# DeltaNet's triangular inverse: two value heads in one product per level, and where the transposes are made

## The reference, cut to what matters

```python
decay = jnp.exp(jnp.where(incl, gc[..., :, None] - gc[..., None, :], -jnp.inf))
kk = jnp.einsum("bhncd,bhnjd->bhncj", k, k)
m = jnp.where(strict, beta[..., :, None] * kk * decay, 0.0) + jnp.eye(C)
rhs = jnp.concatenate([v * beta[..., None], k * (beta * jnp.exp(gc))[..., None]], axis=-1)
sol = lax.linalg.triangular_solve(m, rhs, left_side=True, lower=True, unit_diagonal=True)
```

## Time and profile before

| | |
|---|---|
| time, median of 3 runs | 3418.48 us (3417.89 to 3418.68) |
| profiled execution, first to last instruction | 3413.1 us |
| PE busy | 3254.4 us, 95% |
| VectorE busy | 1421.6 us, 42% |
| ScalarE busy | 910.3 us, 27% |
| GpSimd busy | 1704.4 us, 50% |
| mean granted TensorE clock | 0.989 |

### The profile page before, as it was taken

How to read it: one execution, slowest core, us unless ns; L and a number is a source line. 1 busy time by engine, 2 the same in 40 slices (tenths; PEclk the granted TensorE clock), 3 DMA queues, 4 the chain that set the end, 5 groups by cost and what they waited for, 6 DMA issues and landing times.

```text
span 3413.1 us, 46693 instructions
## 1 busy us (share of the span) xinstructions
PE 3254.4 (95%) x16752; PEld 2712.9 (79%) x16752; DVE 1421.6 (42%) x1929; ACT 910.3 (27%) x1411; POOL 1704.4 (50%) x1748
## 2 busy tenths in 40 slices
PE   8999989999999999999999999999998999999996
PEld 7877878888888888888788887787777878778685
DVE  6722234333433343334331314333356565631723
ACT  5411133333333333333320102111113333310411
POOL 0255634433443344334326777765664555556684
PEclk9999999999999999999999999999999999999998
DMA  6322212211221122112224223222223222223222
GB/s 238 124 85 94 82 55 74 74 55 55 74 74 55 55 74 74 55 55 86 98 69 172 99 91 143 99 92 86 95 97 120 68 88 69 94 91 122 77 96 86
DMA packets 53530, 306.52 MB, mean 90 GB/s; under 512 B 5044, under 2 KB 7220, under 8 KB 21716
## 3 DMA queue, kind: packets, MB, share of 16 engines
q1 hardware_dynamic: 34528, 248.53, 21.2%
q10 hardware_dynamic: 18932, 57.00, 4.5%
HBM read 284.74 MB, written 20.77 MB: 90 GB/s over the span
## 4 chain that ended last, share of the span: by engine, by line
PE 80%; DVE 12%; ACT 5%; issue 2%; DMA 1%; ACTq 0%; DVEq 0%; SPq 0%
PE gemm_ps L436 19%; PE gemm_ps L438 19%; PE gemm_ps L437 19%; DVE arena L878 9%; PE bankC L580 4%; PE bankA L571 3%; ACT arena L1579 2%; PE gemm_ps L795 2%; DVE a_lo L878 2%; PE gemm_ps L797 2%; PE gemm_ps L796 2%; PE bankA L751 2%; PE bankB L587 1%; ACT a_hi L1579 1%; PE bankA L593 1%
## 5 line engine op out<-in xcount | busy, mean ns | idle before, releaser
L436 PE MATMUL gemm_ps<-a_hi,w_hi 128*128 128x512 f32 (+1 forms) x3472 | 1390.8, 401 | 15.4 <-DVE a_lo L878 13.4
L412 POOL CAST w_hi<-w_raw 128x512 fp32r<-128x512 f32 x872 | 547.2, 670 | 1661.9 <-issue 1504.2
L438 PE MATMUL gemm_ps<-a_hi,w_lo 128*128 128x512 f32 (+1 forms) x3472 | 1331.9, 384 | 0.0
L437 PE MATMUL gemm_ps<-a_lo,w_hi 128*128 128x512 f32 (+1 forms) x3472 | 1329.9, 383 | 0.0
L404 POOL TENSOR_TENSOR w_lo<-w_raw,w_hi 128x512 fp32r<-128x512 f32 x872 | 1161.0, 1363 | 4.2
L436 PEld LDWEIGHTS gemm_ps<-a_hi,w_hi 128*128 128x128 f32 x3472 | 657.5, 189 | 145.9 <-DVE a_lo L878 16.3
L438 PEld LDWEIGHTS gemm_ps<-a_hi,w_lo 128*128 128x128 f32 x3472 | 655.4, 189 | 131.2
L437 PEld LDWEIGHTS gemm_ps<-a_lo,w_hi 128*128 128x128 f32 x3472 | 657.5, 189 | 119.2 <-issue 9.0
L878 DVE TENSOR_TENSOR arena<-gemm_ps,arena 128x512 f32<-128x512 f32 (+3 forms) x161 | 107.1, 665 | 615.5 <-PE gemm_ps L438 496.3
L1579 ACT ACTIVATE arena<-arena 128x512 f32<-128x512 f32 (+5 forms) x350 | 214.6, 613 | 397.9 <-DVE arena L878 383.0
L878 DVE RECIPROCAL arena<-arena 128x512 f32<-128x512 f32 (+2 forms) x70 | 172.8, 2468 | 321.7 <-ACT arena L1579 319.7
(11 more groups left out here) (161 smaller groups left out, 2516.6 us busy)
## 6 DMA issues: line engine op xcount, KB each, us to landing
w_raw<-w_stream SPq DMA_DIRECT2D x236, 1024.0 KB, 4.9
y_scratch<-arena ACTq DMA_DIRECT2D x20, 512.0 KB, 3.4
arena<-y_scratch ACTq DMA_DIRECT2D x13, 512.0 KB, 4.3
arena<-gc_scratch ACTq DMA_DIRECT2D x12, 512.0 KB, 3.6
arena<-x_t ACTq DMA_DIRECT2D x2, 2048.0 KB, 10.1
arena<-y_scratch ACTq DMA_DIRECT2D x1, 4096.0 KB, 24.1
x_scratch<-arena ACTq DMA_DIRECT2D x1, 4096.0 KB, 15.7
y_out<-arena ACTq DMA_DIRECT2D x4, 1024.0 KB, 3.9
```

Source lines behind the costliest of these rows:

```text
L412: pool.tensor_copy(part(w_hi, w, q), part(w_raw, w, q)).then_inc(pool_step, 1)
L436: pe.matmul(o, hi, a_hi[:, k, 0:width], start=(k == 0), stop=False)
L437: pe.matmul(o, hi, a_lo[:, k, 0:width], start=False, stop=False)
L438: last = pe.matmul(o, lo, a_hi[:, k, 0:width], start=False, stop=(k == KT - 1))
```

## The change

The two heads share each level's two products. One combined 128x128 matrix per chunk, `pair_n`, holds one head's factor in one triangle and the other head's, transposed, in the other; `inv_b` and `inv_a` hold the pair's inverses in two arrangements. A row operand is brought on by VectorE: a block transposition (`v.transpose`, 128x512), a predicated copy with a mask per partition (`level_rows`) and a copy of the inner columns (`next_level`). TensorE transposes four matrices at three places only: beside the last "whole", in "turn" after level 5, and in "flip" after level 6. The head's scales move: the second head's values are scaled by `v_scale` when they are copied, `kd` and `ke` are made after levels 3 and 4, `dT` after level 1, and `ke` is waited for in "solved". `qd` comes first in "natural". A second reciprocal of `kroot` is kept in PSUM.

```diff
-DN_STEPS = ([("natural", 10), ("values", 8), ("transposed", 6)]
-            + [(s, l, a, w) for l in range(1, LEVELS - 1)
-               for s, a, w in (("half", 0, 0), ("half", 1, 0), ("whole", 0, 0), ("whole", 1, 1), ("turn", 0, 1),
-                               ("turn", 1, 1))]
-            + [(s, LEVELS - 1, a, w) for s, a, w in (("half", 0, 2), ("half", 1, 0), ("whole", 0, 1), ("whole", 1, 0))]
-            + [("solved", 6)]
+DN_STEPS = ([("natural", 12), ("values", 12)]
+            + [(s, l, w) for l in range(1, LEVELS - 2) for s, w in (("half", 1), ("whole", 4))]
+            + [("half", LEVELS - 2, 1), ("whole", LEVELS - 2, 1), ("turn", 3)]
+            + [("half", LEVELS - 1, 1), ("whole", LEVELS - 1, 2), ("flip", 2), ("solved", 4)]
             + [(s, n, g) for n in range(NB) for s, g in (("rest", 2), ("output", 3))]
-            + [("head_out", 28)])
+            + [("head_out", 18)])
...
+        pair_n, turned0 = Nm[:, 0, :, :], Nm[:, 1, :, :]
+        inv_b, inv_a = XT[:, 0, :, :], XT[:, 1, :, :]
+        half_t = T1[:, 0, :, :]
...
+        kinv_ps, ke_ps = (bankB[:, 1, NB * k:NB * k + NB] for k in range(2))
...
+                    pe.wait_ge(s["inv_ready"], 2 * level_count(j, l) - 1)
                     for n in range(NB):
-                        last = pe.matmul(quad(bankA)[:, a, n, :], NmT[:, a, n, :], X[:, a, n, :],
+                        last = pe.matmul(quad(bankA)[:, 0, n, :], pair_n[:, n, :], inv_a[:, n, :],
                                          start=True, stop=True)
...
+                    pe.wait_ge(s["t1_sbuf"], level_count(j, l))
+                    pe.wait_ge(s["inv_ready"], 2 * level_count(j, l))
                     if l == 1:
-                        pe.wait_ge(s["kd_ready"], j + 1)
+                        pe.wait_ge(s["vn_sbuf"], j + 1)
                     for n in range(NB):
-                        last = pe.matmul(quad(bankC)[:, a, n, :], T1[:, a, n, :], XT[:, a, n, :],
+                        last = pe.matmul(quad(bankC)[:, 0, n, :], half_t[:, n, :], inv_b[:, n, :],
                                          start=True, stop=True)
                     last.then_inc(s["dd"], 1)
+                    if l == LEVELS - 1:
+                        for n in range(NB):
+                            pe.transpose(quad(bankB)[:, 1, n, :], inv_a[:, n, :], ident)
+                elif step[0] in ("turn", "flip"):
+                    pe.wait_ge(s["lvl"], 3 * j + (1 if step[0] == "turn" else 2))
                     for n in range(NB):
-                        last = pe.transpose(quad(bankB)[:, a, n, :], XT[:, a, n, :], ident)
+                        last = pe.transpose(quad(bankC)[:, 1, n, :], inv_b[:, n, :], ident)
...
+            def level_rows(l, turned, j):
+                copy_after(v.copy_predicated, chunks(XT, 1), rows[:, l:l + 1].bitcast(U32).to_broadcast([P, T]), turned,
+                           sem=s["inv_ready"], value=2 * level_count(j, l + 1) - 1)
+            def next_level(l, j):
+                level_rows(l, bankC[:, 1, :], j)
+                op(v.tensor_copy, inner(chunks(XT, 0), l), inner(bankB[:, 1, :], l),
+                   sem=s["inv_ready"], value=2 * level_count(j, l + 1))
...
+                    v.wait_ge(s["dd"], level_count(j, l))
+                    late = l >= LEVELS - 2
+                    copy_after(v.copy_predicated, inv_b, both_ways[:, l:l + 1, :].to_broadcast([P, NB, P]),
+                               quad(bankC)[:, 0, :, :], sem=s["lvl"] if late else None, value=3 * j + l - LEVELS + 3)
+                    if late:
+                        return
+                    op(v.transpose, bankC[:, 1, :], chunks(XT, 0))
+                    next_level(l, j)
+                    op(v.transpose, bankB[:, 1, :], chunks(XT, 1))
                     if l == 1:
+                        op(v.tensor_tensor, dT[:, :, :, :], E[:, :, :, :], both(dTm), ALU.mult)
+                    elif l == 2:
+                        op(v.tensor_copy, ke_scale[:, :, 0], cb[:, :, 3, 0])
+                        op(v.tensor_scalar, u_scale[:, :, 0], neg_br[:, :, 0], -1.0, None, ALU.mult)
+                        op(v.tensor_copy, u_scale[:, :, 1], kroot)
+                        op(v.tensor_scalar, neg_k, kroot, -1.0, None, ALU.mult)
+                    elif l == 3:
+                        op(v.tensor_tensor, kd[:, :, :, :], both(by_chunk(bankB[:, 0, :])), by_row(kd_scale), ALU.mult)
                     else:
+                        op(v.tensor_tensor, ke[:, :, :, :], both(by_chunk(bankB[:, 0, :])), by_row(ke_scale), ALU.mult,
+                           sem=s["kd_ready"], value=j + 1)
...
-                    op(t1, t1_ps, ACT.Copy, s["t1_sbuf"], product_count(j, l, a))
+                    op(chunks(T1, 0), bankA[:, 0, :], ACT.Copy, s["t1_sbuf"], level_count(j, step[1]))
+                elif step[0] == "flip":
+                    act.wait_ge(s["turned"], 2 * j + 2)
+                    op(chunks(XT, 1)[0:P // 2, :], bankC[0:P // 2, 1, :], ACT.Copy, s["xt1"], j + 1)
```

More of the change, by code:

```diff
@@ L182, in build @@
         con = sb("con", [P, 4 + 2 * LEVELS, P])
-        ones, ident, incl, reset = (con[:, n, :] for n in range(4))
-        low = con[:, 4:4 + LEVELS, :].bitcast(U32)
+        ones, ident, incl, rows = (con[:, n, :] for n in range(4))
+        both_ways = con[:, 4:4 + LEVELS, :].bitcast(U32)
         lowT = con[:, 4 + LEVELS:4 + 2 * LEVELS, :].bitcast(U32)
@@ L241, in build @@
         kss, kroot, kinv = (at(o_ + 48 + NB * k, NB) for k in range(3))
-        neg_br, pos_br, neg_c, kd_scale = (at(o_ + 60 + 2 * NB * k, 2 * NB).rearrange("p (b a) -> p b a", a=2)
-                                           for k in range(4))
+        neg_br, neg_c, kd_scale, ke_scale, u_scale = (
+            at(o_ + 60 + 2 * NB * k, 2 * NB).rearrange("p (b a) -> p b a", a=2) for k in range(5))
+        v_scale, neg_k = (at(o_ + 60 + 10 * NB + NB * k, NB) for k in range(2))
         q_sq = root
-        assert o_ + 92 <= 20992
+        assert o_ + 60 + 12 * NB <= 20992
         xt = at(BASE, 8192).rearrange("p (k t) -> p k t", k=KT)
@@ L555, in dn_mix @@
                     last.then_inc(s["nat_v"], 1)
[L556 to L562, removed]
-                elif step[0] == "half":
[L564 to L569, removed]
+                elif step[0] == "half":
+                    l = step[1]
+                    pe.wait_ge(s["inv_ready"], 2 * level_count(j, l) - 1)
                     for n in range(NB):
-                        last = pe.matmul(quad(bankA)[:, a, n, :], NmT[:, a, n, :], X[:, a, n, :],
+                        last = pe.matmul(quad(bankA)[:, 0, n, :], pair_n[:, n, :], inv_a[:, n, :],
                                          start=True, stop=True)
@@ L1070, in dn_mix @@
                     op(v.tensor_tensor, neg_br, cb[:, :, 1, :], kinv2, ALU.mult)
                     op(v.tensor_tensor, neg_c, neg_br, kinv2, ALU.mult)
+                    op(v.tensor_scalar, v_scale, neg_br[:, :, 1], -1.0, None, ALU.mult)
                     v.wait_ge(s["pair"], j + 1)
-                    v.wait_ge(s["expd"], 2 * j + 1)
-                    for a in range(2):
+                    for a, to in ((1, pair_n), (0, quad(bankA)[:, 0, :, :])):
                         for n in range(NB):
-                            op(v.scalar_tensor_tensor, NmT[:, a, n, :], bankA[:, 0, n * P:n * P + P],
+                            op(v.scalar_tensor_tensor, to[:, n, :], bankA[:, 0, n * P:n * P + P],
@@ new lines, in dn_mix @@
+                    copy_after(v.copy_predicated, inv_b, both_ways[:, 0:1, :].to_broadcast([P, NB, P]), pair_n)
+                    op(v.transpose, chunks(Nm, 1), chunks(XT, 0))
+                    level_rows(0, chunks(Nm, 1), j)
+                    op(v.tensor_copy, inner(chunks(XT, 0), 0).rearrange("p (n b) t -> p n b t", n=NB),
+                       inner(ident, 0)[:, None, :, :].to_broadcast([P, NB, P // 4, 2]),
+                       sem=s["inv_ready"], value=2 * level_count(j, 1))
+                    op(v.tensor_tensor, kd_scale, cb[:, :, 2, :], kinv2, ALU.mult)
@@ L1083, in dn_mix @@
                            incl, ALU.mult, ALU.mult)
[L1084 to L1093, removed]
-                elif step[0] == "whole":
-                    l, a = step[1:3]
-                    v.wait_ge(s["dd"], product_count(j, l, a))
-                    if l == 1:
-                        changed = (XT[:, a, :, :], lowT[:, l:l + 1, :].to_broadcast([P, NB, P]), quad(bankC)[:, a, :, :])
-                    else:
-                        changed = (level_blocks(chunks(XT, a), l, 1), level_mask(lowT, l, 1),
-                                   level_blocks(bankC[:, a, :], l, 1))
-                    copy_after(v.copy_predicated, *changed, sem=s["lvl"], value=level_count(j, l, a))
@@ new lines, in dn_mix @@
+                elif step[0] == "whole":
+                    l = step[1]
+                    v.wait_ge(s["dd"], level_count(j, l))
[6 more added lines that the diff above has]
```

(23 more changed lines are left out.)

79 lines of the change are left out of this document (32 added, 47 removed).

## The result

The changed kernel takes 3314.69 us (median of 4 runs, 3310.75 to 3320.26) against 3418.18 before; ratio 0.9703, 95% interval 0.9689 to 0.9716. It is faster by 3.0%, and 69 us slower than the 3246 foreseen, outside the range. The profiled execution's span is 3311.8 us.

The account below looks back on a forecast made before the run. PE was taken as the bound, busy 95% of the span. Less PE work (176 us) and removed waits (51), minus new stalls (53) and a later last-trip start (2), gave 172 us off: 3246 us, range 3205 to 3295.

Parts of the forecast that it names:

- VectorE's own load: VectorE's operations summed per level: 5.4 us in level 1, 5.0 in levels 3 and 4, just under the chain's 5.5.
- four small ones together 0.8: Filler among VectorE's operations of a level: four small operations were priced at 0.8 us in all.
- the prediction's own 6.7 for level 2: VectorE from level 2's first copy_predicated through the second tile's convolution: 6.7 us, next result after 5.5, so 1.2 late.
- The trip of 98.5: One trip of the DeltaNet loop was to take 98.5 us after the change, against 113.3 before.
- The stalls: PE's new stalls, 4.4 us a trip, among them 0.5 at the turn, 0.7 for the last tile's convolution, 0.3 for `dT`.
- Fewer products: PE in each trip: 96 product instructions and 36 transpositions fewer, 14.7 us a trip, 176 us in 12 trips.
- The waits before: PE's waits before second products (27.3 us for VectorE, 16.9 for ScalarE) and eight transpositions (7.0) go: 51 us.
- The transposition: VectorE's block transposition of 512 columns in each level's chain, not in the trace, was taken at 0.70 us.
- rival 2: Four-byte transpositions at half rate, 1.2 us each: stalls of 7.0 us a trip, time 3277; chance 0.17.
- Edits taken at nothing: Other edits, such as longer `natural` preparation and shortened `head_out`, were taken as hidden, but for 2 us in the last trip.
- Rival 3: The levels' chain hides wholly, as ScalarE and VectorE react quicker: stalls of 1 us a trip, time 3205; chance 0.10.
- Rival 4: VectorE becomes the bound in four levels, transpositions at 3.35 us: 27 us a trip, time 3517; chance 0.05.

## Why the prediction was wrong

**The step that failed** is in VectorE's own load, level 2: "four small ones together 0.8". The price came from a row of one-input operations, 0.19 each, most of which stand where GpSimd is idle (the one at 1031.02 comes 1.4 us after GpSimd's last subtraction). In level 2 they come just when GpSimd begins its subtractions for the tile that has ended, and each waits for a whole instruction: 5.0 us. The prediction knew the mechanism, and named it for `dT` and for the two-input 128x8 products (0.92 each in the earlier trace rows). But it did not apply it to copies and scales with one input. The trace of before held a sign of it, in a row that the prediction does not use. The small copy behind "natural" took 0.23 us in all trips of the loop but the first, and 0.91 in the first, where it fell among GpSimd's subtractions (448.34 to 455.33):

```profile
453.22 0.91 DVE L1036 COPY arena<-par 128x16 f32 x1 [0.27 <-DVE arena L878]
```

The Trainium skill (SBUF — State Buffer, "SBUF: two separate sides") names both kinds of VectorE operation that an instruction of GpSimd shuts out, those with two SBUF inputs and those in the faster modes that use both ports. For GpSimd's subtractions the traces agree: 1.2 beside GpSimd's subtractions of 1.25, 0.7 beside those of 0.7, 0.17 beside none, 0.16 with the input in PSUM. Beside GpSimd's cast the copy in the trace was not held up (0.17). The page makes no such exception; here the measurement decides, though it is one copy.

**What it led to.** The place was right: "queued behind it is level 3's copy_predicated, for which PE waits at level 4". With 5.0 in place of 0.8 the prediction's own 6.7 for level 2 becomes 10.9, 5.4 beyond its 5.5; the wait measured is 5.3 us a trip, where 1.2 stood. That PE runs at a granted clock of 0.50 behind such a wait was in no term of the sum, and is 21 us. The kernel before had waits of at most 2.4 us in the middle of the loop; behind three of these ten its products slowed too (a clock of 0.69 from 1144 to 1148), and its last trip had a wait of 4.7.

**With the term mended the sum holds.** With the inputs in PSUM, the foreseen operations in the foreseen place at the foreseen price, the time is 3245.1 against 3246. That the two agree to 1 us is in part luck. The trip of 98.5 does not follow from the prediction's own terms, which give 113.3 - 14.7 - 2.4 - 1.5 + 4.4 = 99.1; this kernel's is 98.7. And smaller terms were off against each other. A group of four products for which PE has waited costs 1.00, 0.91 to the next start and 0.09 for the restart, against 0.91 in all; so a level without a wait before it takes 5.7 us, against 5.5. The stalls were overrated: 0.3 at the turn against 0.5, 0.3 behind the last tile's convolution (L590) against 0.7, and next to nothing where `dT` was to come late (1.23 us, since GpSimd is idle there).

**Point by point.** Fewer products: right in count, and the doubled products confirm that PE's time is paid in full. The waits before: those of 27.3 and 16.9 us are gone but for 2.7 in the first trip. Of the 7.0 before the eight transpositions, which the sum took off whole and put back 2, 6.3 stand again before level 1: 3.1 in the first trip, where nothing was foreseen, and 3.2 in the last. The transposition: 0.73 against 0.70; rival 2 did not come. Its argument against, that every other one-input row goes one column a step, overlooks the reciprocal of the earlier trace rows. Edits taken at nothing: `natural` and `head_out` show no wait of PE in the loop but in its first trip (3.1 us for VectorE, 2.7 and 1.4 for ScalarE). That the last trip's tiles' evictions queue behind the levels (3.5 us even with the operations moved) was not foreseen. Rival 3 did not come as one, but better weights reach 3223, between it and the forecast. Rival 4's mechanism, VectorE as the bound with transpositions of 3.35, is out; VectorE did become the bound in one level, by another way. VectorE's busy time was to rise by 12 us a trip and rose by 15.3 (46.4 to 61.7), 11.1 (57.4) with the small operations moved.

## What to carry to other kernels

A small copy or scale from SBUF to SBUF has no price of its own: look up at which moments GpSimd is busy, and price each one there at the length of one GpSimd instruction (1.2 us here instead of 0.17). Put such operations where GpSimd pauses, or give them an input in PSUM; four of them were worth 78 us here. Where an engine waits on an in-order queue, count what stands between the last needed result and the next one, and sum it against the distance of the steps.

## What the runs showed of the hardware

VectorE's block transposition of 128x512 in four-byte data takes 0.727 us to PSUM and 0.712 to SBUF, close to the two-input product with one operand in PSUM (0.69). A one-input copy or scale of VectorE from SBUF to SBUF waited for GpSimd's two-input instructions (1.20 to 1.30 us for 128x4 elements); a reciprocal of that size beside them did not (0.18), and a copy beside GpSimd's cast did not (0.17). A wait of 5.3 us left PE at 1.2 GHz at first (granted clock 0.50 over the 4 us behind it); one of 3.8 us, in the last trip of the kernel with inputs in PSUM, did the same to the products behind it (2.07 us for a group of 1.16). Waits of 2.2 to 2.4 us were followed by such a stretch in 4 of 11 trips of the finer split and in 3 of 10 of the kernel before, and not in the others; waits of 1.0 us in none.
